# Sums of squares of queries and keys: the squares as moving operand, summed into rows and put back by token

## The reference, cut to what matters

```python
def l2norm(x):
    return x * lax.rsqrt(jnp.sum(x * x, axis=-1, keepdims=True) + EPS)

q = l2norm(qkv_c[:, :, 0]) * (GDN_HEAD_DIM ** -0.5)
k = l2norm(qkv_c[:, :, 1])
...
lmat = jnp.where(strict, jnp.einsum('bnhid,bnhjd->bnhij', kb, k) * decay, 0.0)
tinv = lax.linalg.triangular_solve(eye + lmat, ...)          # per chunk of tokens
qk = jnp.where(tril, jnp.einsum('bnhid,bnhjd->bnhij', q, k) * decay, 0.0)
```

## Time and profile before

| | us |
|---|---|
| median of 3 runs | 1192.81 |
| the three runs | 1195.07, 1192.01, 1192.81 |
| span of the profiled execution, first to last instruction | 1187.7 |
| the profiled execution's own time | not listed beside its span |
| TensorE busy | 1016.9 |
| VectorE busy | 399.2 |
| ScalarE busy | 172.8 |
| GpSimd busy | 123.9 |

### The profile page before, as it was taken

One profiled execution on the slowest core, in us unless ns is written; L12 is line 12 of the kernel. 1 busy time (PEld: TensorE's weight loads), 2 busy tenths in 40 slices (PEclk: granted clock), 3 DMA queues, 4 the chain that ended last, 5 costly groups with the idle time before them and its releaser, 6 DMA issues.

```text
span 1187.7 us, 31859 instructions
## 1 busy us (share of the span) xinstructions
PE 1016.9 (86%) x11942; PEld 488.6 (41%) x11943; DVE 399.2 (34%) x1163; ACT 172.8 (15%) x467; POOL 123.9 (10%) x323
## 2 busy tenths in 40 slices
PE   5999999988898688997689998998765899999874
PEld 4778768453333224332233243333212333333321
DVE  2145686863232132231122232222111223232313
ACT  3252314351011001000000011000000000001002
POOL 0140122101001010010000110011000000010100
PEclk9999999989999999999899999999988999999997
DMA  9976839999999999999999997999999999999996
GB/s 325 306 274 228 309 107 334 391 354 421 426 428 428 429 429 427 430 427 430 427 430 427 430 398 327 429 428 429 428 429 428 428 429 428 430 427 429 428 429 276
DMA packets 78102, 463.66 MB, mean 390 GB/s; under 512 B 11675, under 2 KB 31457, under 8 KB 53418
## 3 DMA queue, kind: packets, MB, share of 16 engines
q1 hardware_dynamic: 72927, 461.56, 94.6%
q10 hardware_dynamic: 5139, 1.60, 0.6%
HBM read 455.56 MB, written 7.57 MB: 390 GB/s over the span
## 4 chain that ended last, share of the span: by engine, by line
PE 65%; DMA 18%; DVE 7%; SPq 4%; issue 4%; ACT 1%; DVEq 1%; ACTq 0%
PE psum L673 26%; PE psum L692 14%; DMA weights<-in_w_gu 12%; PE psum L1054 5%; PE psum L648 4%; DMA work<-in_w_down 4%; SPq L952 3%; PE psum L625 3%; PE psum L642 2%; PE psum L1342 2%; PE psum L1017 2%; PE psum L1058 2%; DMA weights<-in_w_ada 1%; DMA work<-l_blocks 1%; DVE work L2443 1%
## 5 line engine op out<-in xcount | busy, mean ns | idle before, releaser
L673 PE MATMUL psum<-weights,work 128*32 128x512 f32 x2928 | 345.6, 612 | 92.5 <-DMA weights<-in_w_gu 46.8
L673 PEld LDWEIGHTS psum<-weights,work 128*32 128x32 f32 x2928 | 92.5, 111 | 311.5 <-issue 239.2
L692 PE MATMUL psum<-weights,work 128*32 128x256 f32 x2624 | 166.1, 405 | 34.3 <-DVE work L2457 31.7
L2443 DVE STREAM_TRANSPOSE work<-psum 128x256 f32<-128x256 f32 x53 | 23.8, 450 | 419.7 <-PE psum L673 416.9
L692 PEld LDWEIGHTS psum<-weights,work 128*32 128x32 f32 x2624 | 85.3, 115 | 109.5 <-issue 65.6
L1859 ACT ACTIVATE work<-work x53 | 22.1, 416 | 503.2 <-DVE work L2447 503.2
L625 PE MATMUL psum<-work 128*32 128x257 f32 (+1 forms) x1296 | 90.5, 393 | 3.2 <-ACT work L1856 3.2
L2467 DVE STREAM_TRANSPOSE work<-work 128x288 f32<-128x288 f32 x53 | 25.3, 478 | 197.0 <-PE psum L648 197.0
L1054 PE MATMUL psum<-work,weights 128*128 128x288 f32 x320 | 82.3, 413 | 0.0
L1054 PEld LDWEIGHTS psum<-work,weights 128*128 128x128 f32 x320 | 60.0, 191 | 17.9 <-issue 2.2
L625 PEld LDWEIGHTS psum<-work 128*32 128x32 f32 (+1 forms) x1296 | 38.3, 111 | 70.5 <-issue 62.1
(11 more groups left out here) (405 smaller groups left out, 905.2 us busy)
## 6 DMA issues: line engine op xcount, KB each, us to landing
weights<-in_w_gu SPq DMA_DIRECT2D x112, 2048.0 KB, 37.0
weights<-in_w_down SPq DMA_DIRECT2D x48, 2048.0 KB, 39.9
work<-in_w_gu SPq DMA_DIRECT2D x16, 2048.0 KB, 36.8
work<-in_w_down SPq DMA_DIRECT2D x16, 2048.0 KB, 43.2
weights<-in_w_ada SPq DMA_DIRECT2D x12, 2048.0 KB, 10.9
weights<-in_w_in SPq DMA_DIRECT2D x5, 2048.0 KB, 14.8
weights<-in_w_out SPq DMA_DIRECT2D x2, 2048.0 KB, 8.2
weights<-in_state_ssm SPq DMA_DIRECT2D x8, 384.0 KB, 5.9
```

Source lines behind the costliest of these rows:

```text
L673: last = mm(bank(GB)[SLOTS * n:SLOTS * n + SLOTS, :].rearrange("p (a x) -> p a x", a=4), xTm[:, k, :], gu[:, k % 2, n], start=k == 0, stop ...
L692: last = mm(bank(YB)[SLOTS * q:SLOTS * q + SLOTS, 0:QW], hT[:, k, :], dn[:, k % 4, QW * q:QW * q + QW], start=k == 0, stop=k == KT - 1)
L2443: v.transpose(features, of_slots[0]).then_inc(s["hid_step"], 1)
```

## The change

The squares become the moving operand. The stationary operand is a window of 32 columns on a small tile (`one_row`) that is zero but for one column of ones, so a matmul writes 32 rows of which one holds the sums of one head, with tokens in columns, and adds zeros to the others. Four groups of 32 rows of PSUM take four heads at once, and up to two heads fall into one group, told apart by the window (`squares_by_row`). ScalarE copies these rows to SBUF (`norm_sb`), and three matmuls with this copy as the stationary operand and a few columns of the identity as the moving one give the sums by token (`sums_by_token`).

Around it: the sample key products move behind those of the first prompt chunk and the sums; the key scales wait for them. After unit 20 the squares come first, so the wait for the samples' inverse stands ahead of `query_products(1, PB)`. All squares of a group are waited for at once. ScalarE's copy stands ahead of the stores of L and behind unit 20's silu. VectorE makes `oeps` in three operations in place of one and clears two small tiles at the start; GpSimd no longer clears `sq_s`. Two semaphores are renamed, since they now count the sums too.

```diff
-            def norms(hs, i):
-
-                for h in hs:
-                    at = QK_ORDER.index(h)
-                    pe.wait_ge(s["sq"], at + 1 + (at >= 8))
-                    for c in range(2):
-                        mm(norm_sum[:, c, h:h + 1], sq[at % 8][:, P * c:P * c + P], ones[:, 0:1], start=True, stop=True)
+            def squares_by_row(i):
+
+                prompts = ((2, 3, 4, 5, 6, 7, 0, 1), (8, 9, 10, 11))[i]
                 pe.wait_ge(s["sq"], (9, 14)[i])
-                at = (H, 0)[i]
-                mm(norm_sum[:, 2, at:at + H], sq_s[i][:, 0:P], ones[:, 0:H], start=True, stop=True)
+                for n, at in enumerate(prompts):
+                    r, j = divmod(n, NQ)
+                    mm(norm_rows[NS * j:NS * j + NS, 0:SEQ], one_row[:, 2 - r:2 - r + NS], sq[at % 8],
+                       start=r == 0, stop=n + NQ >= len(prompts))
                 for h in range(H):
-                    at = (H, 0)[i] + h
-                    last = mm(norm_sum[0:NS, 2, at:at + 1], sq_s[i][:, NS * h:NS * h + NS], ones[:, 0:1], start=True, stop=True)
+                    r, j = divmod(h, NQ)
+                    last = mm(norm_rows[NS * j:NS * j + NS, SEQ:TOK], one_row[:, 2 - r:2 - r + NS], sq_s[i][:, NS * h:NS * h + NS],
+                              start=r == 0, stop=h + NQ >= H)
+                last.then_inc(s["sums_ps"], 1)
+
+            def sums_by_token(i):
+
+                pe.wait_ge(s["sums_read"], 4 + i)
+                rows = ident.rearrange("p (j x) -> p x j", j=NQ)
+                for c in range(3):
+                    n = 1 if i == 1 and c < 2 else 2
+                    last = mm((norm_k, norm_q)[i][:, c, 0:n], norm_sb[:, P * c:P * c + P], rows[:, 0:n, :], start=True, stop=True)
                 last.then_inc(s["norm_ps"], 1)
...
                 if u == 14:
-                    pe.wait_ge(s["dexp"], 1)
-                    norms(QK_ORDER[:8], 0)
+                    pe.wait_ge(s["sums_read"], 3)
+                    pe.wait_ge(s["egates"], 1)
+                    squares_by_row(0)
                     pe.wait_ge(s["s_silu"], 1)
                     pe.wait_ge(s["silu_done"], 8)
-                    key_products(0, None)
                     pe.wait_ge(s["poolT"], 1)
                     key_products(1, PA)
+                    sums_by_token(0)
+                    key_products(0, None)
                     pe.wait_ge(s["poolT"], 2)
                     key_products(2, PB)
...
                 if u == 20:
+                    pe.wait_ge(s["tu_done"], 1)
+                    pe.wait_ge(s["rk2"], 1)
+                    squares_by_row(1)
                     pe.wait_ge(s["silu_done"], 14)
                     pe.wait_ge(s["kv_tok"], 2)
                     query_products(1, PB)
-                    pe.wait_ge(s["tu_done"], 1)
-                    norms(QK_ORDER[8:], 1)
+                    sums_by_token(1)
                     pe.wait_ge(s["s_silu"], 2)
                     query_products(0, None)
...
+                if u in (14, 20):
+                    act.wait_ge(s["sums_ps"], 4 if u == 14 else 5)
+                    act.copy(norm_sb[:, 0:TOK], norm_rows).then_inc(s["sums_read"], 1)
...
                 v.wait_ge(s["norm_ps"], 1)
-                v.wait_ge(s["kk_ps"], 1)
-                own(ts(r2, norm_sum[:, :, H:2 * H], EPS, None, ALU.add))
+                v.wait_ge(s["kk_ps"], 2)
+                own(ts(r2, bank(7)[:, 480:504].rearrange("p (c n) -> p c n", c=3)[:, :, 0:H], EPS, None, ALU.add))
...
-                    own(ts(oeps, norm_sum[:, :, 0:H], EPS * DH, EPS * EPS * DH, ALU.mult, ALU.add))
+                    of_k, of_q = [bank(7)[:, at:at + 24].rearrange("p (c n) -> p c n", c=3) for at in (480, 448)]
+                    for c, lo, hi, sums in ((slice(0, 2), 0, 2, of_k[:, 0:2, H:8]), (slice(0, 2), 2, H, of_q[:, 0:2, 0:4]),
+                                            (slice(2, 3), 0, H, of_q[:, 2:3, 0:H])):
+                        own(ts(oeps[:, c, lo:hi], sums, EPS * DH, EPS * EPS * DH, ALU.mult, ALU.add))
```

More of the change, by code:

```diff
@@ L265, in build @@
         s_tap = DD.at(6384, CT, NS)
-        sq_s = [DD.at(6960 + 288 * i, H * NS + P - NS) for i in range(2)]
+        sq_s = [DD.at(6960 + H * NS * i, H * NS) for i in range(2)]
+        norm_sb = front.at(4 * SOLVE * SOLVE - 3 * P, 3 * P)
         mraw = DD.at(4144, ADA_FIRST, P)
@@ L376, in build @@
         lgT, rfold = sb("logits_T", [P, P])[:, :], sb("fold_of_experts", [P, NE])[:, :]
+        one_row = lgT[:, 0:NS + 2]
         cumf, cnt, cntb = lgT[:, 0:NE + 2], lgT[:, 40:40 + NE], lgT[:, 72:72 + NE]
@@ L451, in prep_out @@
             return heads(pair, P)
-        norm_sum = bank(7)[:, 448:484].rearrange("p (c h) -> p c h", c=3)
+        norm_rows = bank(7)[:, H * NS:H * NS + TOK]
+        norm_k, norm_q = [bank(7)[:, at:at + 24].rearrange("p (c r j) -> p c r j", c=3, j=NQ) for at in (480, 448)]
         gate_sum = bank(7)[:, 256:448]
@@ L1139, in decays @@
                                   start=True, stop=True)
-                last.then_inc(s["diff_ps"], 1)
+                last.then_inc(s["sums_ps"], 1)
             def key_products(o, pair):
@@ L1569, in decay_exp @@
             def decay_exp(o, pair):
-                act.wait_ge(s["diff_ps"], o + 1)
+                act.wait_ge(s["sums_ps"], o + 1)
                 n = ROWS[ORDER[o]]
-                fn(dmat(o)[0:n], prep_out(o, pair), ACT.Exp).then_inc(s["dexp"], 1)
+                fn(dmat(o)[0:n], prep_out(o, pair), ACT.Exp).then_inc(s["sums_read"], 1)
             def evacuate(o, pair, dst, ready, done):
@@ L1912, in _ @@
             v.memset(ab, 0.0)
+            v.memset(norm_sb[:, TOK:3 * P], 0.0)
+            own(v.memset(one_row, 0.0))
+            own(v.memset(one_row[:, 2:3], 1.0))
             v.wait_ge(s["setup_ps"], 1)
@@ L2052, in lower_decays @@
                     n = ROWS[ORDER[o]]
-                    v.wait_ge(s["dexp"], o + 1)
+                    v.wait_ge(s["sums_read"], o + 1)
                     own(tt(dmat(o)[0:n], dmat(o)[0:n], every_head(masks(o)[2][0:n, 0:n], n, n), ALU.mult))
@@ L2066, in l_matrix @@
                 n, c = ROWS[ORDER[o]], ORDER[o]
-                v.wait_ge(s["kk_ps"], o + 1)
+                v.wait_ge(s["kk_ps"], (2, 1, 3)[o])
                 for h in range(H):
@@ L2076, in t_start @@
                 v.wait_ge(s["lmat"], o + 1)
-                v.wait_ge(s["diff_ps"], o + 1)
+                v.wait_ge(s["sums_ps"], o + 1)
                 own(tt(T[0:n], L[0:n], level_mask(o, 0, n), ALU.mult))
@@ L2504, in _ @@
             own(g.memset(uext[:, :, 0:PBUF], 0.0))
-            for i in range(2):
-                own(g.memset(sq_s[i], 0.0))
             flat = blk_t[0:BLOCKS].rearrange("p i j -> p (i j)")
@@ L2536, in _ @@
                 own(ins) if m == 0 else ins.then_inc(s["pooled"], 1)
-            g.wait_ge(s["diff_ps"], 3)
+            g.wait_ge(s["sums_ps"], 3)
             own(g.memset(Tm[0], 0.0))
```

6 lines of the change are left out of this document (3 added, 3 removed).

## The result

| | before | after |
|---|---|---|
| median, us | 1193.94 (1190.56 to 1197.17, 6 runs) | 1200.45 (1196.22 to 1203.98, 6 runs) |
| after to before | | 1.0053, 95% interval 1.0033 to 1.0072 |
| span of the profiled execution | 1187.7 | 1194.1 |

The change makes the kernel some 6 us slower (6.5 us between the medians); 1195.2 us with a range to 1198.5 us was predicted.

What follows compares the result with a forecast made beforehand. Experts run at the pace of their weights, so SyncE's load stream decides: block read +2.0 us, VectorE's extra operations +0.4, together +2.4; span 1190.1 us, with the median 5.1 us above it 1195.2 us, range 1190.5 to 1198.5.

Steps and rivals of the forecast that it cites:

- TensorE at unit 14: First group of sums: 2.1 us saved by fewer matmuls and 1.5 us by a faster clock, so TensorE 3.6 us early.
- the case in which it falls: Clock falls at unit 14 as before, TensorE only 2.1 us early, stores mostly ahead of loads: 1193.6 us, chance 0.10.
- The other signs that were named: Ring loads near 109 us, second store 7 us or more, first block step near 131, TensorE idle at unit 20.
- The collision: After unit 14, earlier ring loads run beside the L stores: 5 to 6 us a store in place of 1.4.
- The 1.4 us that the forecast allows for issue and landing: Part of an L store's 2.8 us landing time that was taken as issue and landing, not packet traffic.
- r: Shift of the read of the L blocks from memory: taken as +2.0 us, bounds -1.7 and +2.4.
- the fourth case: Ring load packets start ahead of the first L store, second store lands at 121 us: 1197.9 us, chance 0.17.
- the third case: Queue turns hold many store pieces, so L stores are undisturbed and the block read comes earlier: 1191.7 us, chance 0.16.
- Unit 20: Second group of sums: 0.8 us more behind the wait, TensorE idle some 4 us, 0.4 us taken for half clock.
- SyncE's path: Block loads and SyncE's queue at the level products: block read's shift plus 0.4 us, so +2.4 us.
- TensorE's own: TensorE's path to the level products: block read's shift plus 0.8 and 0.4 us at unit 20, so +3.2 us.
- The step that failed is the last one: Behind the level products, SyncE's stream of states' and experts' loads decides: +2.4 us reaches the end, span 1190.1 us.

Runs made afterwards that it cites:

- f4: The changed kernel with the edits of e1 and e3, and the query products of chunk 0 put back ahead of unit 20's wait: 1192.65 us, ratio 0.9985.
- f1: The changed kernel with the edits of e1 and e3 together: 1193.77 us, ratio 0.9991 to the kernel before.
- e3: The changed kernel with 8 idle one-column matmuls (16 records) more ahead of unit 20's wait: 1196.09 us, ratio 1.0026 to the kernel before.
- i2: The changed kernel with a short gap in the sample-state loads: three issued, five after two level updates: 1196.17 us, ratio 1.0018 to the kernel before.
- e1: The changed kernel with the ring load behind unit 14 issued only after the third L matrix is finished: 1196.29 us, ratio 1.0024 to the kernel before.
- g4: e3 with the first ring load behind unit 14 issued only after both L stores have landed: 1191.74 us, ratio 0.9972 to the kernel before.
- i1: g4 with a short gap in the sample-state loads: three issued, five after two level updates: 1190.89 us, ratio 0.9976 to the kernel before.
- f3: The changed kernel with only the query products of chunk 0 put back ahead of unit 20's wait: 1205.38 us, ratio 1.0088 to the kernel before.
- g1: f3 with the 8 idle matmuls (16 records) of e3 at unit 20: 1198.31 us, ratio 1.0042 to the kernel before.
- g2: f4 with 24 idle matmuls (48 records) in place of 8 at unit 20: 1193.95 us, ratio 1.0008 to the kernel before.
- g3: The kernel before with 8 matmuls (16 records) fewer in the second group of sums: 1199.82 us, ratio 1.0042 to the kernel before.
- h4: The kernel before with a gap in the sample-state loads that lasted one level update too long: 1202.74 us, ratio 1.0066 to the kernel before.

## Why the prediction was wrong, point by point

**TensorE at unit 14: right.** 3.6 us saved were said, 3.9 measured; L ready at 110.4 us as said. The clock stayed up, so the case in which it falls is out. The other signs that were named came true too (ring loads near 109 us, the second store over 7 us, TensorE idle at unit 20); all of them stand ahead of 181.5 us, and none could show what failed.

**The collision: right in kind, mis-sized, and the sizes cancelled in part.** The second store was to land at 119.3 us and landed at 124.0; the term was 5 to 6 us a store beside the loads, and the pair took 15.1 us from issue instead of 10.4. The first was to end at about 114 us and landed at 117.7, the second 6.3 us behind it. The price of a store came from the read's pieces of 128 bytes, taken as near one for one with pieces of 2 KB. But the rows used for it give 1610 to 2462, about 0.65 to 1, and the stores' pieces of 512 bytes went at 1568 to 2156, about 0.7 to 1. The 1.4 us that the forecast allows for issue and landing stand in no run: the smallest loads nearby, 24 KB, landed in 1.9 and 2.1 us, and a store alone in 2.8. I did not foresee that the late stores hold ScalarE and that the read, issued when the loads are nearly done, lands 4 us faster. Net r was +3.0 where +2.0 was said (bounds -1.7 to +2.4, "beyond neither is excluded"; the fourth case had +4.1).

The page "DMA: Bandwidth & Descriptors" of the Trainium skill (Queues, rings and completion order) has an engine drain a whole packet of one queue before it turns to the next. It does not say how many pieces each of two unlike transfers gets. Here one small piece went for 1.4 pieces of 2 KB: this is against turns that favour the stores, as the third case supposed, and turns of like number on both sides would fit it.

**Unit 20: right.** TensorE waited 2.83 us (4 said), half clock followed (L1163 2.48 us for 1.50), and no cost of it can be measured at the end: f4 is within the noise of f1.

**The level products: 181.5 us said, 181.49 measured.** SyncE's path was to be 2.4 us late and is 3.1 (L821); TensorE's own was to be 3.2 late and is 3.0. That they agree to 0.01 us is luck: the read was 1.0 us later than said, the wait at unit 20 1.2 us shorter.

**The step that failed is the last one:** "The states' and first experts' loads stand in SyncE's queue, and its stream decides, so +2.4 us: span 1190.1 us." It took everything behind the level products as shifted and otherwise the same: +2.4 us, where the medians show 6.5. (That the median lies 5.1 us above the span is no cost of a run, but for the most part the quickness of that one execution; the forecast's difference does not hang on it.) But from 190 us to the experts TensorE waits for other engines only some 5 us in all, in either trace, so a delay of TensorE passes through, and its stop of 1.13 us, a row with "issue" that nobody seemed responsible for, depends on how many instructions come before it and what the DMA engines do at that moment. The change took 16 records away. By e3 and i2 this cost 2.5 to 4 us (0.21 to 0.35% between them and the two measurements of the change), and by e1 against the change and f1 against e3 the stores cost some 3 to 4 us. With both out of the way the kernel is 1 to 3 us faster than before (f1, whose interval includes no change; g4, i1). How much of this is the change's own is not shown, since the kernel before was not run with the same waits and the short gap. No case of mine had the stop; the slowest one, at 1197.9 us, was about the stores alone.

**What stays open.** Why f3's stop was 4.59 us and its median 5 us above the change's, at the same record 55: g1 shows that the time goes away with the stop, not what lengthens it. Why a place earlier than record 39 (g2) did not shorten it. How g3's loss divides between stop and the half clock before the level products. And how long the stop of the kernel before is in most of its executions: its one profile is a quick one, and h4, which was to tell, waited 6.84 us for the states.

## What to carry to other kernels

An edit that makes one engine earlier moves everything that engine releases: look for the transfers it triggers, and put small stores on which a chain waits ahead of large loads with slack, by a wait if need be (g4). If a profile has a stop with no releaser in a dense stretch, treat it as part of the path: count how many instructions an edit adds or removes ahead of it, and try a handful of idle matmuls or a gap in the traffic before judging the edit by its time. An edit that takes work away can be 0.4% slower when it moves such a stop (g3), though how much of that is the stop's is open.

## What the runs showed of the hardware

- TensorE stopped at a fixed count of its instructions: 16 records fewer moved the stop from 39 to 55 (the change, g3), 16 more moved it back (e3, f1, f4), 48 more to 7 (g2). In all twenty traces TensorE went on 1.9 to 3.0 us behind the start of a packet in the queue "instruction" (0.02 MB; in the half microsecond from 186.0 us in the change, TensorE going on at 188.98). The page "Runtime: NRT & Kernel Launch" of the Trainium skill (Instruction fetch mechanics) has instructions fetched in blocks over a DMA queue of the sequencer's own and calls the cost mostly hidden. The trace agrees with the first; the second did not hold here, where stops of 0.47 to 1.41 us remained with a gap in the loads and reached 4.59 us beside them.
- The clock stayed at 2.4 GHz behind the stops of 0.47 to 1.69 us in the last unit and fell to 1.2 GHz behind those of 2.13 to 4.59 us; it also fell behind waits of 2.15 (f4), 2.33 (g3) and 2.34 us (g1) ahead of unit 24's products, and stayed behind one of 1.59 us (e1). The longest half clock, from 192 to 204 us, followed the longest stop (f3).
- Two stores of 384 KB in pieces of 512 bytes landed in 2.8 us each alone (g4), in 2.8 and 9.1 us where the loads left with the second (e1), and in 8.8 and 13.6 us where they left with the first.
